# Sampled attention inside a hybrid decoder step: ranking moved behind the first keys, the near part closed early, last turns and page gates reordered

## The chip, the cores and the metric

The kernel runs on one core of one Trainium2 chip. The time is the device time of one execution in microseconds; lower is better.

## The reference

The program computes one inference step of a two-layer decoder for two groups that share the weights: one prompt of 256 tokens and 8 samples of 4 tokens with 2048 past tokens each. Each layer projects its input into a state-space group and an attention group of 8 query heads over 2 key/value heads. The attention has three branches: compressed blocks, the best 16 of 33 blocks of 64 past keys, and a window of 512. Cut to the selection and the three weighted sums:

```python
score = jnp.einsum('bktc,jc->bktj', p_cmp, overlap)
score = jnp.where(forced, FORCED_SCORE, jnp.where(causal, score, -1.0))
_, idx = lax.top_k(score, min(N_SEL, n_blocks))
...
o_slc = sel_attend(q, gather_selected_sample(cache_slc_kv, layer, page_table, kv_slc, idx), idx, pos)
...
o_win, _ = dense_gqa(q, kv_all[..., 0, :], kv_all[..., 1, :], d.astype(jnp.float32), (d >= 0) & (d < WINDOW))
...
attn = gates[..., 0:1] * o_cmp + gates[..., 1:2] * o_slc + gates[..., 2:3] * o_win
```

The samples' rows are the 128 combinations of sample, head of a key/value head, and step.

## The kernel before

The program is written by hand, one instruction stream for each engine, with semaphores between them; the order of the work is the order of the code. A loop runs the layer twice. In each layer come the input projection with the state-space scan, the compression of the cached pages (a long row of convolution matmuls), the attention stage that this change concerns, the output projection and the feed-forward network, whose matmuls (L1046) are most of TensorE's time.

In the attention stage TensorE, VectorE and ScalarE work on the prompt's 8 heads (two buffers, `a` and `b_`, heads in turn) and on the samples at once:

- **Keys.** Twenty sets of keys of about 1 MB or less, numbered 0 to 19, pass through a ring of four buffers. Sets 0 to 3 are the window's, 4 to 19 the past's 2048 positions. Even sets are asked for by SP, odd ones by GpSimd (POOL), eight pages of 128 KB each, when the set four places ahead has been used (`kring_free`). `keys(n, e)` (L869) multiplies set 2n+e into bank 2; VectorE's `window_out` and `keys_out` (L1669) add the position bias, write the result to SBUF and free the bank (`kgroup_evac`). The window's scores are the near part `SW` (2 x 544 columns), the past's are the far part `SS` (2 x 2080 columns), the compressed branch's are `SCM`.
- **Ranking.** VectorE counts for each of 33 blocks how many beat it, with ties broken by a table that GpSimd's queue loads (`tie_in`), and writes a mask of blocks (`RNK`, L1731 and L1733). TensorE spreads it over the rows in `mask()`, VectorE adds it in `masked(i)` to 512 columns at a time and takes their maximum.
- **Prompt heads.** For head n: `scores` on TensorE; `prompt_bias` on VectorE (L1743 to L1753: bias, maxima); `prompt_exp` on ScalarE; `prompt_scale` on VectorE (L1758 to L1768); `turn_p` on TensorE (8 transposes, L904 to L908) and `turned` on ScalarE (L1289 to L1291); `weigh` on TensorE (L917 to L921); `prompt_out` on VectorE (L1772) for two heads at once. `prompt_bias` of a head waits for `turn_p` of the head two before it.
- **End of the samples' scores.** `sample_exp` on ScalarE (L1296) makes the exponentials of `SW`, then of `SS`; VectorE gates and normalises them (L1837 to L1850); TensorE transposes them in 12 turns of up to two 128-column blocks (L980), ScalarE copies each turn to SBUF (L1316, L1320). Turns 0 to 8 hold the far part, the second half of turn 8 and turns 9 to 11 the near and the compressed one. Their order is the list `TURNS`, their banks go round a ring of six.
- **Values.** For each of the 8 samples (batches) b, TensorE multiplies the transposed weights by 16 pages of values and the window's values (L999). Three buffers hold the pages: the key ring, weight slot 0, and the memory of `SS` itself (index 1 in `VB`), which batch 2 is the first to use. SP, GpSimd and ScalarE each ask for a third of its pages (L354). Loads of later batches wait until the batch before them in the same buffer is done (`vring_free`). Between the batches TensorE sums squares for the two output norms (L571, L1025), which ScalarE makes. The output projection's first weights are loaded in the same stretch.

The order before: VectorE ranks right after the first window half. The near part's maximum, exponentials and scaling come at the very end, with the far part's, after head 7's scaling. ScalarE makes the far exponentials behind the evacuations of heads 6 and 7. TensorE turns heads 6 and 7, then three near turns, weighs heads 6 and 7, then does the nine other turns. Batch 2's pages wait for the last turn (`st_done` 12).

## Time and profile before

| | us |
|---|---|
| median of 3 runs | 3471.27 |
| lowest and highest | 3469.81, 3475.97 |
| the profiled execution, its own time | 3474.08 |
| span of its trace | 3472.5 |
| TensorE matmul busy in it | 3222.8 (93%) |
| VectorE busy | 1855.5 (53%) |
| ScalarE busy | 1232.9 (36%) |
| mean granted TensorE clock | 0.965 |

The attention stage lies at about 587 to 766 us in the first layer and 2314 to 2495 us in the second. A timeline row gives the start, the duration from there to the end of what is merged in it, the engine, the line, the operation with its tensors, and in square brackets how long the engine sat idle before it and what ended that. DVE is VectorE, ACT ScalarE, PE TensorE; a q behind a name is that engine's sequencer, which carries out waits, drains and DMA issues. The granted clock is a share of 2.4 GHz.

### The profile page before, as it was taken

To read this page: it belongs to the slowest core of one execution; us is meant where nothing else is said; L and a number is where in the kernel's file an instruction comes from. 1 tells how busy PE (TensorE), PEld (TensorE's weight loads), DVE (VectorE), ACT (ScalarE), POOL (GpSimd) and SP (SyncE) were. 2 spreads that over 40 slices of the span, in tenths; PEclk is the share of its full clock that TensorE was granted. 3 is DMA by queue.
4 is the path that set the end of the run, shared out by engine and by line. 5 is a ranking of instruction groups with operands and counts; after the bars stand their busy time and mean duration, and the time that the engine had idled before them with its cause. 6 is when DMAs were issued, how large, how long until landed. Compare 5 with 4: busy or idle time off the path is not lost. (4 is left out here: it accounts for less than half of the span.)

```text
span 3472.5 us, 56544 instructions
## 1 busy us (share of the span) xinstructions
PE 3222.8 (93%) x21882; PEld 2904.9 (84%) x21882; DVE 1855.5 (53%) x2703; ACT 1232.9 (36%) x1534; POOL 313.1 (9%) x556
## 2 busy tenths in 40 slices
PE   6899998769999999999979999987699999999998
PEld 4677777559999999999956777765599999999998
DVE  4887565734444444444448875656344444444444
ACT  2121453423333333333322124534233333333332
POOL 0001233430000000000000011324200000000000
PEclk8999999879999999999989999998899999999999
DMA  4524555764444444444234244656644444444443
GB/s 159 215 84 155 183 184 178 224 243 158 157 158 169 169 163 156 164 169 151 116 133 190 97 173 155 206 161 220 242 151 165 169 158 159 166 169 151 164 170 124
DMA packets 141468, 579.77 MB, mean 167 GB/s; under 512 B 21009, under 2 KB 91314, under 8 KB 115570
## 3 DMA queue, kind: packets, MB, share of 16 engines
q1 hardware_dynamic: 105282, 472.09, 36.9%
q0 software_dynamic: 26528, 76.84, 6.5%
q10 hardware_dynamic: 9488, 28.71, 2.1%
q8 instruction: 90, 1.47, 0.2%
q14 instruction: 80, 0.66, 0.1%
HBM read 570.02 MB, written 24.18 MB: 171 GB/s over the span
## 5 line engine op out<-in xcount | busy, mean ns | idle before, releaser
L1046 PE MATMUL banks<-normed_hi,weights_hi 128*128 128x288 f32 x4224 | 1251.5, 296 | 5.3 <-DVE ffn_hidden L1420 3.4
L1046 PE MATMUL banks<-normed_lo,weights_hi 128*128 128x288 f32 x4224 | 1246.1, 295 | 0.0
L1046 PE MATMUL banks<-normed_hi,weights_lo 128*128 128x288 f32 x4224 | 1241.9, 294 | 0.0
L1420 DVE TENSOR_TENSOR weights_lo<-weight_slots,weights_hi 128x2048 fp32r<-128x2048 f32 x296 | 686.7, 2320 | 990.9 <-ACTq L1345 990.4
L1342 ACT ACTIVATE weights_hi<-weight_slots 128x2048 fp32r<-128x2048 f32 x296 | 566.9, 1915 | 1101.1 <-PE banks L1046 1099.4
L1046 PEld LDWEIGHTS banks<-normed_hi,weights_hi 128*128 128x128 f32 x4224 | 791.5, 187 | 6.4 <-DVE ffn_hidden L1420 3.8
L1046 PEld LDWEIGHTS banks<-normed_hi,weights_lo 128*128 128x128 f32 x4224 | 795.5, 188 | 0.0
L1046 PEld LDWEIGHTS banks<-normed_lo,weights_hi 128*128 128x128 f32 x4224 | 792.9, 188 | 0.2
L646 PE MATMUL banks<-normed,weight_slots 128*128 128x288 f32 x1664 | 440.6, 415 | 8.9 <-DMA weight_slots<-in_w_in 8.9
L646 PEld LDWEIGHTS banks<-normed,weight_slots 128*128 128x128 f32 x1664 | 322.5, 195 | 103.0 <-issue 13.0
L835 PE MATMUL banks<-conv_high,conv_weights 128*128 128x508 f32 x1024 | 331.3, 405 | 14.3 <-DVE conv_low_b L1420 9.3
L835 PEld LDWEIGHTS banks<-conv_high,conv_weights 128*128 128x128 f32 x1024 | 192.6, 190 | 67.9 <-DVE conv_low_b L1420 16.1
L372 DVE TENSOR_TENSOR arena<-arena 128x256 f32<-128x256 f32 (+4 forms) x576 | 221.5, 388 | 29.8 <-issue 0.9
L1258 ACT ACTIVATE conv_high<-arena 128x512 fp32r<-128x512 f32 x256 | 157.9, 628 | 170.6 <-PE banks L835 170.4
L1046 PE MATMUL banks<-mixed_hi,weights_hi 128*128 128x288 f32 x512 | 158.3, 309 | 12.0 <-DVEq L1884 12.0
L339 POOL DMA_DIRECT2D arena<-in_cache_cmp x256 | 137.6, 538 | 282.6 <-issue 256.0
L1046 PE MATMUL banks<-mixed_lo,weights_hi 128*128 128x288 f32 x512 | 154.6, 302 | 0.0
L1046 PE MATMUL banks<-mixed_hi,weights_lo 128*128 128x288 f32 x512 | 154.0, 301 | 0.0
L1103 ACT ACTIVATE projected<-banks 128x576 f32<-128x576 f32 x28 | 18.2, 649 | 310.2 <-PE banks L646 290.9
L1420 DVE TENSOR_TENSOR conv_low_a<-arena,conv_high 128x512 fp32r<-128x512 f32 x128 | 86.5, 690 | 73.0 <-ACT conv_high L1258 71.7
L1420 DVE TENSOR_TENSOR conv_low_b<-arena,conv_high 128x512 fp32r<-128x512 f32 x128 | 87.6, 691 | 67.2 <-ACT conv_high L1258 65.9
L1046 PEld LDWEIGHTS banks<-mixed_hi,weights_hi 128*128 128x128 f32 x512 | 99.6, 195 | 13.3 <-issue 12.6
(298 smaller groups left out, 3036.3 us busy)
## 6 DMA issues: line engine op xcount, KB each, us to landing
weight_slots<-in_w_gu SPq DMA_DIRECT2D x88, 2048.0 KB, 7.5
weight_slots<-in_w_down SPq DMA_DIRECT2D x44, 2048.0 KB, 7.6
weight_slots<-in_w_in SPq DMA_DIRECT2D x28, 2048.0 KB, 8.3
arena<-in_cache_cmp SPq DMA_DIRECT2D x256, 128.0 KB, 4.1
arena<-in_cache_cmp POOLq DMA_DIRECT2D x256, 128.0 KB, 4.1
weight_slots<-in_w_out SPq DMA_DIRECT2D x16, 2048.0 KB, 7.6
out_win_kept<-in_win_rows ACTq DMA_DIRECT2D x2, 8128.0 KB
arena<-in_cache_slc_v SPq DMA_DIRECT2D x76, 128.0 KB, 5.1
```

The source lines that it names most:

```text
L339: eng.dma_start(AR[:, o:o + 256], T["cache_cmp"][bass.ds((lay * 160 + page) * 2 + k, 1)] .rearrange("a p x -> p (a x)")).then_inc(S[f"raw{ ...
L372: return eng.tensor_tensor(out, a, b, op)
L646: mm = pe.matmul(PS[s][:, m, 0:TOK], WR[:, s, c, 128 * m:128 * m + 128], hc(c), start=c == 0, stop=c == KC - 1)
L835: mm = pe.matmul(acc, w, x, start=i == hf == 0 and x is hi and w is wh, stop=i == 15 and hf == 1 and x is lo)
L1046: mm = pe.matmul(out, wt[:, hf, col], x[:, rhs + c, :], start=begin and c == 0 and i == 0, stop=hf == 1 and c == k - 1 and i == 2, skip_gr ...
L1103: act.activation(dst, src, ACT.Copy).then_inc(S[sem], by)
L1258: act.activation(HRG[:, n % 4, :].rearrange("p (g x) -> p g x", x=16), RAW[u % 2][:, :, i, :], ACT.Copy)\
L1342: w = act.activation(WH[:, hf, :], WR[:, s, 8 * hf:8 * hf + 8, :].rearrange("p a b -> p (a b)"), ACT.Copy)
L1420: return dve.tensor_tensor(out, a, b, op)
```

## The change

On VectorE, the ranking moves from behind the first window half to behind the second key part (the new function `rank`). The window's second half moves between heads 0 and 1. The near maximum is closed right behind it, and the gating of the compressed part and the scaling of the near part move from the end to between heads 2 and 3. The mask's copy moves behind `keys_out(1, 0)`. At the end, the far maximum is taken ahead of `prompt_out(4)` and the far part is scaled between heads 6 and 7. The instructions are the same, with one small reduction split in two.

On TensorE, `mask()` moves behind the first two heads' weighing, the three near turns move ahead of head 6's turn, and head 7's turn goes between far turns; both weighings follow the last turn. The turns' banks are a ring of four (0, 1, 4, 5), so that banks 6 and 7 stay with the heads. On ScalarE, the near exponentials follow those of heads 0 and 1, the far ones stand ahead of the evacuations of heads 6 and 7. The pages of batch 2 wait one by one for the turn that empties their columns.

```diff
+            TURNS = [9, 10, 11, 8] + list(range(8))
+            def turned_off(x):
+                ends = [(w - k * NS) // P // 2 for k, w in ((w // NS, w) for w in (256 * x, min(256 * x + 255, 2 * NS - 1)))]
+                return max(TURNS.index(n) for n in ends) + 1
...
-                if not last:
-                    eng.wait_ge(*((S["kring_free"], 22), (S["st_done"], 12), (S["kring_free"], 22))[VB[b]])
+                if not last and VB[b] != 1:
+                    eng.wait_ge(S["kring_free"], 22)
                 for x, page in zip(mine, p):
+                    if not last and VB[b] == 1:
+                        eng.wait_ge(S["st_done"], turned_off(x))
...
-            TURNS = [9, 10, 11] + list(range(9))
+            TURN_BANKS = [0, 1, 4, 5]
...
                 half_group(0, 0)
-                mask()
                 half_group(0, 1)
...
                 turn_and_weigh(0, ((1, 0),))
+                mask()
...
+                pe.wait_ge(S["ps_max"], NQ)
+                pe.wait_ge(S["sw_ready"], 1)
+                for i in range(3):
+                    turn_s(i)
+                turn_p(6, a)
+                pe.wait_ge(S["sw_ready"], 2)
+                for i in range(3, 8):
+                    turn_s(i)
+                turn_p(7, b_)
+                for i in range(8, 12):
+                    turn_s(i)
+                weigh(6, a, 1)
+                weigh(7, b_, 1)
...
+                prompt_exp(0, a)
+                prompt_exp(1, b_)
+                act.wait_ge(S["sw_max"], 1)
+                sample_exp(1, SW)
...
+                for i in range(3):
+                    turned_s(i)
+                act.wait_ge(S["sw_max"], 2)
+                sample_exp(0, SS)
+                turned(6, a)
+                for i in range(3, 8):
+                    turned_s(i)
+                turned(7, b_)
+                for i in range(8, 12):
+                    turned_s(i)
...
                 prompt_bias(0, a)
+                window_out(1)
                 prompt_bias(1, b_)
-                window_out(1)
                 dve.tensor_reduce(mxw[:, :, 0], SW[:, :, 0:WIN], AXX, ALU.max)
...
                 keys_out(0, 1)
+                rank()
                 prompt_bias(2, a)
+                gated_compressed()
+                for k in range(NKV):
+                    sample_scale(1, k, SW)
+                dve.drain().then_inc(S["sw_ready"], 1)
                 prompt_bias(3, b_)
                 keys_out(1, 0)
+                dve.wait_ge(S["mask_done"], 1)
+                dve.tensor_copy(MB, PS[3][:, :, 256:288])
...
+                dve.drain()
+                dve.tensor_reduce(SM[:, 54:56], mxs, AXX, ALU.max)
...
                 prompt_out(4)
                 prompt_scale(6, a)
+                for k in range(NKV):
+                    sample_scale(0, k, SS)
+                dve.drain().then_inc(S["sw_ready"], 1)
                 prompt_scale(7, b_)
+                prompt_out(6)
```

Two places in the instruction order. VectorE behind the first window half (the row of two 128x256 parts), before: the ranking, then head 0's bias.

```order
L1669 SCALAR_TENSOR_TENSOR arena<-consts,banks 128x256 x2
L1420 TENSOR_TENSOR arena<-arena 64x1089 x2
L1731 TENSOR_REDUCE arena<-arena 64x33
L1733 TENSOR_SCALAR arena<-arena 64x33
L1743 SCALAR_TENSOR_TENSOR weight_slots<-consts,banks 128x512
L1743 SCALAR_TENSOR_TENSOR weight_slots<-consts,banks 128x256
L1746 SCALAR_TENSOR_TENSOR weight_slots<-consts,banks 128x30
L1750 TENSOR_REDUCE smalls<-weight_slots 128x2 x3
L1753 TENSOR_SCALAR smalls<-smalls 128x6
```

VectorE after, from the second key part on (line numbers are those of the changed kernel: L1695 is the key part, L1759 to L1769 a head's bias, L1823 the gating, L1829 to L1835 the near part's scaling).

```order
L1695 SCALAR_TENSOR_TENSOR arena<-consts,banks 128x256 x2
L1446 TENSOR_TENSOR arena<-arena 64x1089 x2
L1812 TENSOR_REDUCE arena<-arena 64x33
L1814 TENSOR_SCALAR arena<-arena 64x33
L1759 SCALAR_TENSOR_TENSOR weight_slots<-consts,banks 128x512
L1759 SCALAR_TENSOR_TENSOR weight_slots<-consts,banks 128x256
L1762 SCALAR_TENSOR_TENSOR weight_slots<-consts,banks 128x30
L1766 TENSOR_REDUCE smalls<-weight_slots 128x2 x3
L1769 TENSOR_SCALAR smalls<-smalls 128x6
L1823 TENSOR_SCALAR arena<-arena,gates_sample 128x127 x2
L1829 TENSOR_SCALAR smalls<-smalls 128x1
L1831 RECIPROCAL smalls<-smalls 128x1
```

The ranking now stands three parts (a window half and two key parts), two head biases and two head scalings later, and the near part's scaling follows head 2's bias.

ScalarE at the end of the stage, before: near exponentials (544 columns), evacuations of heads 6 and 7, far exponentials (2080 columns), then the turns.

```order
L1296 ACTIVATE arena,smalls<-arena,smalls 128x544 x2
L1289 ACTIVATE weight_slots<-banks 128x512
L1290 ACTIVATE weight_slots<-banks 128x256
L1291 ACTIVATE weight_slots<-banks 15x256
L1289 ACTIVATE weight_slots<-banks 128x512
L1290 ACTIVATE weight_slots<-banks 128x256
L1291 ACTIVATE weight_slots<-banks 15x256
L1296 ACTIVATE arena,smalls<-arena,smalls 128x2080 x2
L1316 ACTIVATE arena<-banks 128x512
```

ScalarE after, the same place (L1321 and L1325 copy the samples' turns, L1309 makes the exponentials, L1302 to L1304 evacuate a head).

```order
L1321 ACTIVATE arena<-banks 128x512
L1325 ACTIVATE arena<-banks 128x256
L1325 ACTIVATE arena<-banks 32x256
L1321 ACTIVATE arena<-banks 127x256
L1309 ACTIVATE arena,smalls<-arena,smalls 128x2080 x2
L1302 ACTIVATE weight_slots<-banks 128x512
L1303 ACTIVATE weight_slots<-banks 128x256
L1304 ACTIVATE weight_slots<-banks 15x256
L1325 ACTIVATE arena<-banks 32x256
L1325 ACTIVATE arena<-banks 128x256
L1321 ACTIVATE arena<-banks 128x512 x4
```

The three near turns are copied ahead of the far exponentials, and head 6's evacuation now follows these.

## Rows read from the trace of the kernel before

**Rows 1.** Waits of TensorE over the whole span: us in total, times, longest.

```profile
PE banks L869 <- DVEq L1723: 27.6, 4, 12.4
```

**Rows 2.** Timeline of VectorE, first part of the stage; the last row is layer two.

```profile
602.49 2.65 DVE L1420 TENSOR_TENSOR arena<-arena 64x1089 f32<-64x1089 f32 x2 [3.62 <-DMA arena<-in_ties]
...
606.93 1.14 DVE L1743 SCALAR_TENSOR_TENSOR weight_slots<-consts,banks 128x512 f32<-128x512 f32 x2 [0.19 <-issue]
...
609.59 1.14 DVE L1743 SCALAR_TENSOR_TENSOR weight_slots<-consts,banks 128x512 f32<-128x512 f32 x2
...
621.65 0.87 DVE L1669 SCALAR_TENSOR_TENSOR arena<-consts,banks 128x256 f32<-128x256 f32 x2 [1.38 <-PE banks L869]
626.23 1.14 DVE L1743 SCALAR_TENSOR_TENSOR weight_slots<-consts,banks 128x512 f32<-128x512 f32 x2 [3.71 <-PE banks L908]
...
635.30 0.68 DVE L1772 COPY normed<-banks 128x512 f32<-128x512 f32 x1
...
2365.41 0.68 DVE L1772 COPY normed<-banks 128x512 f32<-128x512 f32 x1
```

**Rows 3.** Timeline of TensorE, key sets 4 to 7; the last row is layer two.

```profile
613.25 3.64 PE L869 MATMUL banks<-arena 128*32 128x256 f32 x32 [12.27 <-DVEq L1723]
...
618.00 3.58 PE L869 MATMUL banks<-weight_slots,arena 128*32 128x256 f32 x32 [0.54 <-DVEq L1779]
...
2340.84 3.64 PE L869 MATMUL banks<-arena 128*32 128x256 f32 x32 [12.36 <-DVEq L1723]
```

**Rows 4.** Single page loads of L327 on SP, each with its time to landing.

```profile
L327 SPq DMA_DIRECT2D arena<-in_cache_slc_k x1: 333/333/333, 596.0 to 596.0; - x1
...
DMA to landing us min/median/max: 12.4/12.4/12.4
...
L327 SPq DMA_DIRECT2D arena<-in_cache_slc_k x1: 333/333/333, 2323.4 to 2323.4; - x1
...
DMA to landing us min/median/max: 15.9/15.9/15.9
...
DMA to landing us min/median/max: 8.6/8.6/8.6
```

**Rows 5.** Timeline of VectorE, end of the samples' scores, first layer.

```profile
675.40 0.17 DVE L1832 TENSOR_SCALAR smalls<-smalls 128x4 f32<-128x4 f32 x1
...
679.75 0.48 DVE L1837 TENSOR_SCALAR arena<-arena,gates_sample 128x127 f32<-128x127 f32 x2
...
682.52 0.50 DVE L1850 TENSOR_SCALAR arena<-arena,smalls 128x544 f32<-128x544 f32 x1 [0.42 <-issue]
...
688.45 0.15 DVE L1844 TENSOR_SCALAR smalls<-smalls 128x1 f32<-128x1 f32 x1 [0.22 <-ACTq L1298]
```

**Rows 6.** Timeline of ScalarE, the first half of the far exponentials.

```profile
684.05 2.03 ACT L1296 ACTIVATE arena<-arena,smalls 128x2080 f32<-128x2080 f32 x1
```

**Rows 7.** Timeline of TensorE, turns, weighings and first batch; the last row is layer two.

```profile
677.57 0.47 PE L904 MATMUL banks<-consts,weight_slots 128*128 128x128 f32 x1 [8.01 <-DVEq L1768]
...
683.20 2.37 PE L980 MATMUL banks<-consts,arena 128*128 128x128 f32 x10 [0.39 <-DVEq L1853]
...
691.16 4.15 PE L980 MATMUL banks<-consts,arena 128*128 128x128 f32 x36 [1.12 <-DVEq L1853]
698.43 0.41 PE L999 MATMUL banks<-ssm_out,arena 127*32 127x128 f32 x4 [3.13 <-ACTq L1322]
...
702.96 5.25 PE L571 MATMUL banks<-squares,consts 128*128 128x288 f32 x16
...
2433.09 5.09 PE L571 MATMUL banks<-squares,consts 128*128 128x288 f32 x16 [1.47 <-ACT squares L566]
```

**Rows 8.** Stretches: length, busy us (count) PE, PEld, DVE, ACT, POOL, clock, DMA share, GB/s.

```profile
677.50:685.40 7.90, 6.12 (x27) 4.96 (x28) 4.14 (x18) 3.57 (x7) 0.00 (x0) 0.50 0.64 217
691.10:695.30 4.20, 4.14 (x36) 3.89 (x36) 0.00 (x0) 2.77 (x5) 0.00 (x0) 1.00 0.01 2
...
724.00:762.00 38.00, 21.02 (x385) 17.32 (x381) 3.12 (x7) 4.12 (x3) 8.72 (x12) 0.68 0.88 327
```

More of the change, by code:

```diff
@@ L1283, in prompt_exp @@
                     act.drain().then_inc(S["p_exp"], 1)
-                for j, h in enumerate(HEADS):
-                    prompt_exp(j, h)
                 def turned(n, h):
@@ L1298, in sample_exp, with turned_s @@
                         act.drain().then_inc(S["sw_exp"], 1)
-                for i in range(3):
-                    for j, h in enumerate(HEADS):
-                        turned(2 * i + j, h)
-                    for j, h in enumerate(HEADS):
-                        prompt_exp(2 * i + 2 + j, h)
-                act.wait_ge(S["sw_max"], 1)
-                sample_exp(1, SW)
-                for j, h in enumerate(HEADS):
-                    turned(6 + j, h)
-                sample_exp(0, SS)
                 widths = [P] * 16 + [SMP] + [P] * 4 + [SMP] + [NCMP]
-                for i, n in enumerate(TURNS):
+                def turned_s(i):
                     act.wait_ge(S["st_done"], i + 1)
+                    n = TURNS[i]
                     w = widths[2 * n:2 * n + 2]
-                    src = bank([0, 1, 4, 5, 6, 7][i % 6])
+                    src = bank(TURN_BANKS[i % 4])
                     if len(set(w)) == 1:
@@ L1322, in _ @@
                     act.drain().then_inc(S["st_evac"], 1)
+                a, b_ = HEADS
+                prompt_exp(0, a)
[3 more added lines that the diff above has]
+                for i in range(3):
+                    for j, h in enumerate(HEADS):
+                        turned(2 * i + j, h)
+                    for j, h in enumerate(HEADS):
+                        prompt_exp(2 * i + 2 + j, h)
+                for i in range(3):
+                    turned_s(i)
[7 more added lines that the diff above has]
+                    turned_s(i)
                 values(act, 2, "rest")
@@ L1725, in _ @@
                 window_out(0)
-                dve.wait_ge(S["tie_in"], 16)
-                tt(sel[1], sel[1], sel[2], ALU.mult)
-                dve.drain()
-                tt(sel[0], sel[0], sel[1], ALU.add)
-                dve.drain()
-                dve.tensor_reduce(RNK, sel[0], AXX, ALU.add)
-                dve.drain()
-                dve.tensor_scalar(RNK, RNK, float(NSEL), MASKED, ALU.is_ge, ALU.mult)
-                dve.drain().then_inc(S["ranked"], 1)
                 d1, dcp, slh = const(K_D1), const(K_DCP), const(K_SLH)
```

82 lines of the change are left out of this document (40 added, 42 removed).

## The prediction

> **What bounds the kernel now.** I read the waits of TensorE first, then the timelines of the attention stage, engine by engine. [rows 1]: over the two layers TensorE waits 27.6 us for one line of VectorE, L1723, the drain behind a window or key part. The timelines place it: per layer one wait of about 12.3 us before key set 4 [rows 3]; later one of 8.01 us before the seventh head's turns, and 3.13 us before the value products [rows 7]. VectorE is what TensorE waits for and is itself nearly full: from the third head's bias at 626.23 to the first head output at 635.30 there is no gap worth naming [rows 2]. So a removed TensorE wait is worth only what VectorE's own chain gets shorter. Times below are of the first layer; the second repeats them 1727.6 us later (the wait for set 4 ends at 613.25 and 2340.84), and 1730.1 later from 635.30 and 2365.41 on [rows 2, 3].
>
> **Early part: ranking and near part.** Before, VectorE waits 3.62 us for the tie table, ranks from 602.49 to 606.74 (4.25 us), and only then does heads 0 and 1 (2.66 us each, 606.93 to 609.59) and the second window half [rows 2]. In the new order, from 598.87 (602.49 less the wait): bias 2.7, window half 1.0, bias 2.7, the near maximum 1.7, scale 2.1, so VectorE is free at 609.1. The window half frees the key bank at 602.7 instead of 613.2, ten microseconds earlier.
>
> That is not the gain, because the keys are not there. Set 4's last page, issued at 596.0, lands 12.4 us later, at 608.4; in the second layer 2323.4 plus 15.9, 2339.3 [rows 4]. So TensorE starts it at 608.4 and 2339.3 against 613.25 and 2340.84: 4.8 and 1.5 us. Its 32 matmul records take 3.64 [rows 3], at the 1.2 GHz level ("cold" below, a granted clock of 0.50 as in the first of [rows 8]; 1.00 is 2.4 GHz, "warm"): done at 612.1 and 2342.9. Set 6's last page, issued at 605.4, lands 8.6 later, at 614.0 (the last line of [rows 4]). The next two sets take 3.58 us where they stood before [rows 3], done at 617.6 against 621.6; in the second layer I take 2.7, between 3.58 and a warm half of it, from 2343.9: 2346.6.
>
> Then VectorE: key part 1.0 (L1669, 0.87 and its drain), rank 4.25: 622.9 and 2351.9. Ranking now stands where VectorE before waited 3.71 us for the first turn (626.23) [rows 2]. From the end of set 7 to that turn's end it took 626.1 less 621.6, 4.5 us; from 617.6 that gives 622.1, so the turn is just ready and the rank hides in it. From 626.23 to 635.30 everything stays: 9.07 us. Added into it are the gating and the near part's two scalings, 679.75 to 683.02, 3.3 us [rows 5], and the mask's copy, 0.3 (an estimate from the 0.68 of the 512-column copy). Sum: 622.9 + 12.7 = 635.6 against 635.30, a **loss of 0.3**; second layer 2351.9 + 12.7 = 2364.6 against 2365.41, a **gain of 0.8**. The early rearrangement as a whole is about zero: VectorE is work-conserving there, and 3.3 us moved in uses up the waits taken out. Bounds: if the sets start no sooner than before, the loss is 3.7 per layer (rank 4.25 plus 3.6 less the 3.71 wait and about 0.4); if set 6 runs at the warm clock, a gain of 1.5. I take the middle since set 4's landing is a row. Behind 635.30 the order of VectorE is unchanged until the last mask add; that stretch keeps its length.
>
> **Late part.** The last maximum no longer waits for the head copy (0.68) and the near one: ready at 674.55 against 675.57 [rows 5]. ScalarE before did the near exponentials, then turns 6 and 7, and began the 2080-column exponential at 684.05 [rows 6]. Now near exponentials are long done and this one starts at 674.6, **9.4 us earlier**. Two halves at 2.2 each end at 676.8 and 679.0. VectorE has copied the heads and scaled head 6 (2.1, as from 675.5 to 677.57) at 677.3, and scales the halves, 1.95 each (688.45 to 690.4) [rows 5]: 679.3 and 681.3. TensorE did the three near turns (10 transposes) while VectorE masked, so they and their evacuations cost nothing; they are covered by the 8.01 us wait, of which 4 us would have to go before they showed. Head 6's turn (from 677.4, 1.9 us) ends before 681.3 too.
>
> From 681.4 on, TensorE's sum: 20 transposes of the far part, cold, 4.5 (10 took 2.37 at 683.20); head 7's turn, 8 transposes, 1.2, between 0.9 warm and 1.9 cold by the same two rows; 16 transposes warm 1.85 (36 took 4.15 at 691.16); the two last weighings 4.65 (685.4 to 690.04, partly cold) [rows 7]. That is 12.2: the value products start at 693.6 against 698.43. ScalarE is not later: before, its evacuations trailed the last transpose by 3.1 us (695.31 to 698.43), and now 4.65 us of weighing stand there. Gain **4.8**. The weighings and a turn, which lay in a gap before, now stand in the path: that is why 9.4 shrinks to 4.8. Then the first batch: it took 4.53 us (698.43 to 702.96) after its 3.13 us wait, but 3.1 in the second layer (698.43 plus 1730.1 to 2431.6), which then waited 1.47 for squares until 2433.09 [rows 7]. Now there is no wait ahead (TensorE comes warm) and ScalarE's squares are 7 us earlier, so both layers save 1.45 more. **Late gain 6.25 per layer**, 12.5 in all. Bounds: all warm (2.3 + 0.9 + 1.85 + 4.15, with the batch's 1.45) 9.3 per layer; all cold (4.7 + 1.9 + 3.8 + 7, the weighings estimated as 1.5 times theirs here) about zero.
>
> **The bank ring** shrinks from six to four; ScalarE's pace was 0.8 a turn (691.16 to 698.43, nine turns), under the 0.9 of four cold transposes, so it costs nothing above this sum. **The gates of the value pages** free pages 0 and 3 some 5 us before the last turn, the rest with it. In the old trace nobody waits for the third batch's pages: they were asked from 695.5 and used at 717.66; now they are asked by 689 and wanted near 711. I price the gates at zero; cover is the 20 us of batches 0 and 1.
>
> **What follows.** Every later load is released by a batch that TensorE has finished, so its release moves with TensorE. From 724 to 762 the DMA engines are 88% busy at 327 GB/s [rows 8]. The Trainium skill, page "Trainium Kernel Development and Optimization", Key Constraints, says that DMAs of SP, ACT and POOL "all run on the same 16 DMA engines and interleave"; by that rule earlier issue by itself cannot shorten this tail, only an earlier start can. The trace agrees with that reading at 88%, and the sum does not rest on it: the start is earlier here. The FFN behind it is unchanged.
>
> **Sum.** 12.5 + 0.8 - 0.3 = 13.0 us. The profiled execution took 3474.1 (span 3472.5); it gives 3461. Against the median of 3471.27 it gives **3458**.
>
> **Rivals.** A: the early part loses its bound. Sets 6 and 7 or the turns come later than I reckon and VectorE's added 3.3 us is paid fully, 3.7 per layer. For it: VectorE's density, and landings of 12.4 and 15.9 us that show a crowded DMA [rows 4]. Against: sets 4 to 7 are asked at the same times as before. 13.0 less (3.4 + 4.5) leaves 5: **3466**.
>
> B: the tail gives it back. The value pages and output weights of the last four batches take the DMA's time whatever TensorE does, and the gain ends as a longer wait for pages. For: [rows 8]. Against: at 88% it has some room, and each page is asked when TensorE has freed its place, so the whole tail starts earlier. Only the warm batch and 1 to 2 us remain: **3469**.
>
> C, slower: TensorE's clock. The new order leaves TensorE idle from about 671 to 677 and again for 2 us before the long row of transposes. If it then stays at the 1.2 GHz level to the first batch, the late path has 17.4 us instead of 12.2 and no gain; if set 6, the score products and first turns are cold too (3.5 us later than reckoned), the early part loses 3.8 and 2.7. It decides from the point where both the transposes and the weighings run cold: 3471.3 + 6.5 = **3478**. For it: from 677.5 to 685.4 the granted clock is 0.50, after 8 us of idling [rows 8]. Against: one row of weighings later, from 691.1 to 695.3, it is 1.00, in spite of 1.1 us of idling between [rows 7, 8]. The Trainium skill, "TensorE: Matmul & The Clock Gate", Part 1, says that "the default state is throttled, and activity releases the throttle", which speaks against the longer idling here; by it the long transposes would start cold, which is what I charge, and then warm. The trace agrees: 10 transposes in 2.37 at 0.50 and 36 in 4.15 at 1.00 [rows 7, 8].
>
> **How the numbers follow.** Forecast 0.64 (3452 to 3464); A 0.18 (3463 to 3469); B 0.10; C 0.08. A measurement of this kernel tells about 0.2% (7 us) from no change: faster is below 3464.3, the forecast and half of A, 0.73; same is half of A, B and a little of C, 0.20; slower 0.07. For 8 in 10 the range takes the forecast with its warm bound (3449) and most of A: 3449 to 3469.
>
> **What would show it.** Right: set 4's keys start at landing, near 608 and 2339, not at 603; the first head output near its old place (within 1.5 us); the 2080-column exponential about 9 us earlier; value products 4 to 7 us earlier; waits for value pages of the old size. Wrong: a VectorE gap before the third head's bias (A), longer page waits in the tail (B), transposes and weighings at the clock of 1.2 GHz throughout (C). If the first head output comes 3 us or more earlier, I have overcharged the moved near part.

## The result and the profile after

The changed kernel took 3458.01 us (median of 10 runs, 3450.33 to 3465.15) against 3473.16 us for the kernel before (10 runs beside them, 3469.81 to 3477.86): a ratio of 0.9954, with a 95% interval of 0.9946 to 0.9963. Run once more on another chip, it gave 0.9945 [0.9933, 0.9957]. The forecast of 3458 us holds. The profiled execution took 3458.01 us, with a span of 3456.4 against 3472.5 before, 16.1 us less.

Waits of TensorE in the changed kernel over the whole span, those of the attention stage that matter here (waited for: us in total, times, longest us):

```profile
PE banks L1014 <- DMA arena<-in_cache_slc_v: 18.6, 6, 8.5
PE banks L878 <- DVEq L1795: 15.2, 6, 3.8
PE banks L913 <- DVEq L1784: 13.5, 2, 6.7
PE banks L878 <- DMA arena<-in_cache_slc_k: 12.9, 2, 7.5
...
PE banks L1014 <- DMA weight_slots<-in_cache_slc_v: 8.7, 2, 4.5
...
PE banks L981 <- DVEq L1892: 4.1, 2, 2.1
...
PE banks L878 <- DMA weight_slots<-in_win_k: 2.6, 1, 2.6
...
PE banks L878 <- DMA weight_slots<-in_cache_slc_k: 1.9, 1, 1.9
...
PE banks L878 <- DVEq L1749: 1.5, 1, 1.5
```

Of the 27.6 us of [rows 1] 1.5 are left (L1749 is the old L1723). In their place TensorE waits 14.8 us for key pages, where it waited 2.4 before, and 2.6 us for a window page. The waits for value pages are what they were, 27.3 us in sum against 28.0. L878 is the old L869, L1014 the old L999, L981 the old L980.

Timeline of TensorE in the changed kernel, first layer: start of the stage (L859) and key sets 4 to 7, the lines that answer to [rows 3] (start us, us, engine and line, operation, and in brackets the idle time before it and what ended it). A row of 32 records holds two key sets, and is called here by the first of them: "set 4" is sets 4 and 5, "set 6" is 6 and 7.

```profile
589.91 1.08 PE L859 MATMUL banks<-projected,arena 128*32 128x127 f32 x32 [0.70 <-issue]
...
611.37 3.64 PE L878 MATMUL banks<-arena 128*32 128x256 f32 x32 [5.38 <-DMA arena<-in_cache_slc_k]
616.13 3.64 PE L878 MATMUL banks<-weight_slots,arena 128*32 128x256 f32 x32 [1.12 <-DVEq L1795]
```

The stage starts at 589.91 here and at 587.16 in the execution before (2310.48 and 2314.32 in the second layer), so I count from that start. Set 4 begins at 21.46 instead of 26.09. VectorE, the lines that answer to [rows 2] and [rows 5] (ranking's reduction, first head output, last maximum):

```profile
623.55 1.28 DVE L1812 TENSOR_REDUCE arena<-arena 64x33 f32<-64x1089 f32 x1
...
637.26 0.68 DVE L1788 COPY normed<-banks 128x512 f32<-128x512 f32 x1
...
676.58 0.17 DVE L1887 TENSOR_SCALAR smalls<-smalls 128x2 f32<-128x2 f32 x1
```

The first head output stands at 47.35 against 48.14 us from the stage's start, and in the second layer at 48.07 against 51.09. ScalarE and TensorE at the end of the stage, the lines that answer to [rows 6] and [rows 7]:

```profile
676.78 2.03 ACT L1309 ACTIVATE arena<-arena,smalls 128x2080 f32<-128x2080 f32 x1 [1.28 <-DVE smalls L1887]
```

```profile
671.34 1.31 PE L981 MATMUL banks<-consts,arena 128*128 128x128 f32 x10
...
683.42 4.45 PE L981 MATMUL banks<-consts,arena 128*32 128x128 f32 x20 [2.08 <-DVEq L1892]
...
689.22 1.91 PE L981 MATMUL banks<-consts,arena 128*128 128x128 f32 x16
...
695.13 0.41 PE L1014 MATMUL banks<-ssm_out,arena 127*32 127x128 f32 x4
```

Stretches of the changed kernel (length, busy us of PE, PEld, DVE, ACT, POOL with counts, clock, DMA share, GB/s):

```profile
683.40:688.20 4.80, 4.78 (x23) 4.72 (x24) 1.80 (x8) 2.73 (x6) 0.54 (x1) 0.50 0.23 79
689.20:691.00 1.80, 1.80 (x19) 1.80 (x18) 0.00 (x0) 1.48 (x4) 0.53 (x1) 1.00 0.18 57
```

The reader sees the far exponential 86.87 us from the stage's start instead of 96.89. Twenty transposes follow at a granted clock of 0.50 (1.2 GHz), 0.22 us each, and then sixteen at 1.00 (2.4 GHz), 0.12 us each. The value products begin at 105.22 against 111.27. Nothing is given back later: the output projection starts at 172.14 against 179.05, and at 170.05 against 180.99 in the second layer. The two layers save 6.91 and 10.94, 17.85 in sum; the rest of the program differs by 1.8 us the other way.

### The profile page after: what moved, and what is told of

Its sections match the earlier page's. It is cut to its first block, busy times and chain, and to the rows that moved or that the text cites. A ratio compares the mean times of both kernels' runs of the same rounds, so it can differ in the third digit from the quotient of the medians.

```text
span 3456.4 us, 56548 instructions
## 1 busy us (share of the span) xinstructions
PE 3225.8 (93%) x21882; PEld 2905.8 (84%) x21882; DVE 1857.0 (54%) x2705; ACT 1233.0 (36%) x1534; POOL 313.2 (9%) x556
## 4 chain that ended last, share of the span: by engine, by line
PE 42%; DVE 3%; DMA 2%; ACT 1%; issue 1%; DVEq 1%; ACTq 0%; SPq 0%; PEld 0%; PEldq 0%
PE banks L1061 27%; PE banks L655 5%; PE banks L844 4%; DMA weight_slots<-in_w_in 1%; PE banks L645 1%; PE banks L632 1%; DMA arena<-in_cache_slc_v 1%; PE banks L878 1%; DMA weight_slots<-in_cmp_w 0%; DVE arena L1446 0%; DVE weights_lo L1446 0%; DMA weight_slots<-in_cache_slc_k 0%; PE banks L624 0%; PE banks L693 0%; PE banks L1014 0%
## 5 line engine op out<-in xcount | busy, mean ns | idle before, releaser
L381 DVE TENSOR_TENSOR arena<-arena 128x256 f32<-128x256 f32 (+4 forms) x576 | 221.7, 388 | 29.9 <-issue 0.9
```

The lines of the kernel that those rows point to most:

```text
L381: return eng.tensor_tensor(out, a, b, op)
```

## The experiments

Places below are microseconds from the start of the stage, first layer and second, each read from the profiled execution of the kernel: the first head output, the first 80 value products of a batch, and the start of the output projection. Ratios are against the kernel before on the same chip. (The value products that began at 105.22 and 111.27 above are the batch's first four records; its row of 80 follows 0.7 us later.)

| kernel | ratio, 95% interval | first output | value products | projection |
|---|---|---|---|---|
| before | 1 | 48.1, 51.1 | 112.0, 114.9 | 179.1, 181.0 |
| changed | 0.9954 [0.9946, 0.9963] | 47.4, 48.1 | 105.9, 106.3 | 172.1, 170.1 |
| e0_changed_again | 0.9945 [0.9933, 0.9957] | 46.7, 47.9 | 106.2, 108.8 | 171.1, 174.8 |
| e1_rank_first | 0.9977 [0.9967, 0.9986] | 52.5, 50.4 | 111.9, 108.9 | 176.5, 173.9 |
| e2_early_alone | 0.9996 [0.9987, 1.0004] | 48.6, 48.7 | 112.2, 112.4 | 177.4, 177.5 |
| e3_gates_back | 0.9951 [0.9939, 0.9964] | 51.0, 48.2 | 109.2, 106.4 | 173.4, 170.8 |
| e4_near_in_wait | 0.9956 [0.9941, 0.9972] | 44.7, 44.5 | 105.2, 103.3 | 171.3, 167.2 |
| e5_kept_warm | 0.9967 [0.9955, 0.9979] | 47.0, 47.7 | 102.8, 103.5 | 172.8, 173.1 |
| e6_table_later | 0.9961 [0.9948, 0.9975] | 49.0, 48.5 | 108.4, 106.4 | 173.0, 170.4 |
| e9_near_mid_warm | 0.9945 [0.9932, 0.9959] | 44.8, 44.2 | 101.4, 101.0 | 168.3, 166.0 |
| e10_all_warm | 0.9928 [0.9915, 0.9942] | 44.4, 44.9 | 98.7, 99.1 | 163.5, 163.2 |
| e11_kept_warm_fewer | 0.9961 [0.9948, 0.9973] | 49.4, 48.5 | 107.3, 106.2 | 175.1, 172.2 |
| e12_early_mid_warm | 0.9918 [0.9905, 0.9931] | 44.9, 45.2 | 101.9, 101.9 | 168.6, 167.9 |
| e13_all_warm_again | 0.9916 [0.9902, 0.9931] | 45.7, 44.7 | 99.7, 98.7 | 163.9, 163.8 |

The changed kernel once more on another chip, as a measure of what two executions differ by:

> The changed kernel once more, unchanged, on the chip of the next two runs, as what they are compared with. Theory: ratio to the kernel before 0.9954 within 0.0008. Rival (the gain depends on the chip): a ratio outside 0.9945 to 0.9963.

Measured: 0.9945, at the edge between the two; 3456.7 us against 3458.0. The two executions agree within about 1 us in the first layer and differ by 2.6 us at the second layer's value products and by 4.8 at its projection. Part of the 2.6 is seen: in the second layer of the repeat set 12 followed a wait of 2.44 us and took 3.56, where it took 1.94 in the changed kernel. So a single place is read to 3 to 5 us, and only durations and waits of single rows, and the time between two neighbouring rows, are read closer.

**The ranking's place.** `rank()` goes back ahead of the first heads' scores, and the near part stays early:

```
                 window_out(0)
+                rank()
...
                 keys_out(0, 1)
-                rank()
                 prompt_bias(2, a)
```

> The changed kernel with the ranking back at its old place, right behind the first window half; all else as changed. My theory (VectorE is work-conserving in the early part, and the ranking's new place fills the wait for the third head's turn): the window half frees the key bank some 8 us later, set 4 starts near 613 instead of near 611 and the ranking no longer fills VectorE's wait, so each layer is 3 us longer: about 6 us over the changed kernel, ratio to the kernel before 0.9970 to 0.9975. Rival (keys were bound by their landing, the move gives nothing): the same time as the changed kernel, 0.995. Rival (the move is where all the early gain comes from, set 4's start moves 5 us and passes through): 10 us, 0.998 or more.

Measured: 0.9977, and the wait for VectorE before set 4 is back. TensorE of e1_rank_first:

```profile
612.75 3.19 PE L878 MATMUL banks<-arena 128*32 128x256 f32 x32 [9.41 <-DVEq L1749]
620.21 3.64 PE L878 MATMUL banks<-weight_slots,arena 128*32 128x256 f32 x32 [4.27 <-DVEq L1808]
```

The first output comes 5.2 and 2.3 us later than in the changed kernel. The interval, 0.9967 to 0.9986, excludes the first rival (0.995) and not the second (0.998). Moving the ranking behind the keys is therefore worth about half of the whole change, as long as the near part stands early.

**The early part alone.** Ranking and near part as in the changed kernel, but the last turns on ScalarE and TensorE and the end of VectorE's order as before: the far scaling and its signal stand behind the last head's, and the far maximum behind `prompt_out(4)`. On VectorE, against the changed kernel:

```
+                prompt_out(4)
...
-                prompt_out(4)
                 prompt_scale(6, a)
+                prompt_scale(7, b_)
                 for k in range(NKV):
                     sample_scale(0, k, SS)
+                prompt_out(6)
                 dve.drain().then_inc(S["sw_ready"], 1)
-                prompt_scale(7, b_)
-                prompt_out(6)
```

> The kernel before with the early part of the change alone: ranking behind the second key part, near maximum, near exponentials, gating and near scaling early, the mask's product behind the first weighings; the end of the stage in the old order (heads 6 and 7 turned and evacuated, then the far exponentials, six banks, pages of batch 2 at the last turn). My theory as predicted: the early part gives about zero up to the first head output, and as the trace of the changed kernel shows it, 0.8 us in the first layer and 3.0 in the second; nothing after it but the near maximum's 0.2 us. So about 4 us under the kernel before, ratio 0.9985 to 0.9995. Rival (the near part's 3.3 us was on the end's path before, and its leaving the end is a gain of its own): another 3 us or more per layer, ratio 0.997 or less.

Measured: 0.9996, no change; the rival, a gain of its own at the stage's end, is out. The first output is at its old place in the first layer (48.57 against 48.14) though TensorE starts set 4 at 21.74 instead of 26.09; in the second it comes 2.4 us earlier (48.72 against 51.09), no more than two executions differ by. This was the prediction's claim: the ranking's removal from the wait pays for the 3.3 us of near part moved in, and no more. The two experiments fit together if the ranking's move is the cover of the near part: without it (e1_rank_first) the first output is 4.4 us later than before the change in the first layer, though 0.7 earlier in the second. The late part alone was not run, so what the late order brings is the difference between this run and the whole change, 0.9996 to 0.9954, and not a run of its own.

**The gates.** Page gates of the value loads as before:

```
-                if not last and VB[b] != 1:
-                    eng.wait_ge(S["kring_free"], 22)
+                if not last:
+                    eng.wait_ge(*((S["kring_free"], 22), (S["st_done"], 12), (S["kring_free"], 22))[VB[b]])
...
-                    if not last and VB[b] == 1:
-                        eng.wait_ge(S["st_done"], turned_off(x))
```

> The changed kernel with the page gates of batch 2 undone: all its pages wait for the last turn again. My theory: nobody waits for these pages, the cover is the 20 us of batches 0 and 1, so the same time as the changed kernel, ratio 0.995 to 0.996. Rival (the early pages take load from the crowded tail): 2 us or more slower than the changed kernel, and longer waits for pages in batches 4 to 7.

Measured: 0.9951 against 0.9954 for the change: the gates turn by turn are worth nothing that can be measured. The value products of the third batch did not wait for pages in either, in either layer.

**The near part in a real gap.** In the changed kernel VectorE idles before the last keys of the middle pair of heads (`keys_out(2, 1)`), 2.67 us in the first layer and 3.76 in the second (the expectation says 3.8 for both). The near scaling goes there:

```
-                gated_compressed()
-                for k in range(NKV):
-                    sample_scale(1, k, SW)
-                dve.drain().then_inc(S["sw_ready"], 1)
                 prompt_bias(3, b_)
...
                 keys_out(2, 0)
+                gated_compressed()
+                for k in range(NKV):
+                    sample_scale(1, k, SW)
+                dve.drain().then_inc(S["sw_ready"], 1)
                 keys_out(2, 1)
```

> The changed kernel with the gating and the near part's scaling moved from between heads 2 and 3 to just ahead of VectorE's write of the key sets 14 and 15, where VectorE waits 3.8 us for TensorE in both layers. My theory (VectorE's chain sets the early part, each us of work in it counts and work in a wait is free): the third head's chain up to the first head output is 2.9 us shorter per layer and the moved work vanishes in the wait: 5 to 6 us faster than the changed kernel, ratio 0.9937 to 0.9942. Rival (TensorE or the key landings bound the stretch once VectorE is lighter): under 2 us gained, ratio 0.995. Rival (the work lands in front of a bank that TensorE waits for): slower than the changed kernel.

Measured: 0.9956, a miss; nothing was gained beyond the change. The timeline of TensorE tells where it went. First e4_near_in_wait, the key sets of the middle (10, 12 and 14), then the same sets in the changed kernel:

```profile
630.72 1.93 PE L878 MATMUL banks<-weight_slots,arena 128*32 128x256 f32 x32 [0.19 <-DVEq L1795]
...
639.44 3.51 PE L878 MATMUL banks<-arena 128*32 128x256 f32 x32 [2.13 <-DVEq L1795]
...
647.75 3.64 PE L878 MATMUL banks<-weight_slots,arena 128*32 128x256 f32 x32 [3.78 <-DVEq L1795]
```

```profile
634.46 3.58 PE L878 MATMUL banks<-weight_slots,arena 128*32 128x256 f32 x32 [2.55 <-DVEq L1795]
...
643.50 1.93 PE L878 MATMUL banks<-arena 128*32 128x256 f32 x32 [0.92 <-DVEq L1795]
...
650.23 2.45 PE L878 MATMUL banks<-weight_slots,arena 128*32 128x256 f32 x32 [3.78 <-DVEq L1795]
```

The granted clock in sets 12 and 14 of e4_near_in_wait, then in set 12 of the changed kernel (length, busy us of PE, PEld, DVE, ACT, POOL with counts, clock, DMA share, GB/s):

```profile
639.50:642.90 3.40, 3.40 (x33) 1.50 (x33) 2.52 (x7) 0.00 (x0) 0.00 (x0) 0.53 0.28 94
647.80:651.30 3.50, 3.50 (x32) 1.49 (x32) 2.16 (x10) 2.41 (x12) 0.51 (x1) 0.50 0.74 248
```

```profile
643.50:645.40 1.90, 1.90 (x33) 1.12 (x33) 1.81 (x4) 0.23 (x1) 0.00 (x0) 1.00 0.75 233
```

The stages start at 588.80 and 589.91. Set 12 of e4_near_in_wait begins at 50.64, 2.95 us ahead of the changed kernel's (53.59). But it follows a wait of 2.13 us instead of 0.92 and takes 3.51 us instead of 1.93, so it ends 1.37 ahead; set 14 takes 3.64 instead of 2.45 and ends 0.18 ahead. The time won on VectorE became a longer idle on TensorE, and the slower matmuls behind it used it up. In the second layer sets 12 and 14 took 2.77 and 3.30 us, and of 4.1 us of lead at set 12 3.0 were kept to the value products. That is no more than two executions differ by.

**TensorE kept busy in the middle.** To e4_near_in_wait, transposes of the identity whose results nobody reads are added in the waits before sets 12 and 14. They write bank 6, so they wait until ScalarE has emptied it. `keep_on` is new:

```
+                def keep_on(count, n=2):
+                    for x in range(count):
+                        pe.transpose(bank(n)[:, 128 * (x % 4):128 * (x % 4) + 128], ident, ident)
...
-                turn_and_weigh(1, ((2, 0), (2, 1)))
+                turn_p(2, a)
+                pe.wait_ge(S["pt_evac"], 4)
+                keep_on(8, 6)
+                half_group(2, 0)
+                turn_p(3, b_)
+                pe.wait_ge(S["pt_evac"], 5)
+                keep_on(20, 6)
+                half_group(2, 1)
+                weigh(2, a, 0)
+                weigh(3, b_, 0)
```

> The kernel with the near block of the sampled heads moved into the wait ahead of the last keys of set group 2 (label e4_near_in_wait), and in it 8 and 20 transposes of the identity into bank 6 (read by nobody) ahead of the two key sets between turn_p(2) and weigh(2). In e4_near_in_wait the first key set of the stretch came 2.95 us earlier from the stage's start than in the changed kernel, but the two sets took 3.51 and 3.64 us behind waits of 2.13 and 3.78 us, against 1.93 and 2.45, and the lead was 1.37 us behind the one and 0.18 us behind the other. My theory (the 1.2 GHz clock after these waits takes the lead back): both sets take 1.93 us, the value products start 2 to 2.9 us earlier from the stage's start than in e4_near_in_wait (105.2 and 103.3 us there), ratio about 0.9940. Rival (VectorE's own work between the sets sets the pace, and faster sets only make TensorE wait longer for the bank): the sets take 1.93 us, the waits ahead grow by as much, value products within 0.7 us of e4_near_in_wait, ratio 0.9955.

Measured: the sets take 1.93 us each, with no wait between the added transposes and set 14; the granted clock of both is 1.00 (second block):

```profile
639.95 1.93 PE L878 MATMUL banks<-arena 128*32 128x256 f32 x32
...
644.13 2.40 PE L937 MATMUL banks<-consts 128*128 128x128 f32 x20 [1.23 <-ACTq L1320]
646.68 1.93 PE L878 MATMUL banks<-weight_slots,arena 128*32 128x256 f32 x32
```

```profile
640.00:641.80 1.80, 1.80 (x33) 0.86 (x32) 1.72 (x4) 0.00 (x0) 0.00 (x0) 1.00 0.50 172
646.70:648.60 1.90, 1.90 (x33) 1.14 (x33) 1.53 (x9) 1.90 (x9) 0.54 (x1) 1.00 0.93 314
```

The value products come at 101.4 and 101.0 instead of 105.2 and 103.3: 3.8 and 2.3 us, about as expected. The ratio of 0.9945 overlaps the 0.9956 of e4_near_in_wait, and these places overlap what executions differ by; what carries the verdict is the time from row to row. From the start of set 12 to that of set 14 it is 6.73 to 6.74 us in every execution of this order in which set 12 took 1.93 to 1.94, and 8.31 to 8.37 in those in which it ran slow (both layers of e4_near_in_wait, the second of e0_changed_again); e9_near_mid_warm is back at 6.73 and 6.74. From set 14 to set 16 it is 6.13 and 6.12 us here against 8.60 and 7.49. The two stretches give 4.05 us back in the first layer and 3.00 in the second. The clock, then, and not VectorE, took the lead back: had VectorE set the pace, as the rival says, the starts would not have moved.

**TensorE kept busy before the far turns.** On the changed kernel:

```
                 for i in range(3):
                     turn_s(i)
+                pe.wait_ge(S["kgroup_evac"], 11)
+                keep_on(40)
                 turn_p(6, a)
+                keep_on(16)
```

> The changed kernel, with 40 transposes of the identity into a free bank (their result is read by nobody) between the first six near and cached turns of the sampled heads and turn_p(6), and 16 more behind turn_p(6), so that TensorE does not idle before the 20 far transposes. In the changed kernel those 20 took 4.45 us behind waits of 2.08 us, and 16 behind them 1.91 us. My theory (the clock level after an idle is what they cost): the 20 take about 2.4 us, the value products start 2.0 us earlier in each layer, ratio to the kernel before about 0.9942 (changed kernel alone 0.9954). Rival one (ScalarE and VectorE, which empty the banks of the turns, set the pace): the transposes get faster but wait in between, the value products start no more than 0.5 us earlier, ratio 0.9953. Rival two (the added transposes are still running when the far scores are ready): the value products start later, ratio 0.996 or more.

Measured: 0.9967, no better than the change and above its interval at the middle, though the transposes did what was expected. TensorE, then ScalarE of e5_kept_warm:

```profile
680.66 2.36 PE L981 MATMUL banks<-consts,arena 128*32 128x128 f32 x20 [1.20 <-DVEq L1901]
...
690.33 2.39 PE L1023 MATMUL banks<-arena 128*32 128x128 f32 x80
695.10 6.47 PE L580 MATMUL banks<-squares,consts 128*128 128x288 f32 x16 [2.37 <-ACT squares L575]
```

```profile
690.43 4.12 ACTq L363 DMA_DIRECT2D arena<-in_cache_slc_v  x5
694.60 0.78 ACT L575 ACTIVATE squares<-normed 128x288 f32<-128x288 f32 x2 [5.85 <-issue]
```

The transposes took 2.36 us for 4.45, and the value products came 3.1 and 2.7 us earlier. Then TensorE waited 2.37 and 2.50 us for the squares, and both normalisations ran slow (6.47 and 6.41 us where the changed kernel has 5.09; the granted clock over the first was 0.73 for 1.00). ScalarE's page issues began only 2.2 and 1.8 us earlier than in the changed kernel, since its evacuations now bind, and the five of them took 4.12 and 4.25 us in place of 2.42, which used up what was left. The lead is gone at the second batch: it began at 114.0 and 114.8, the changed kernel's at 113.3 and 113.6. The third batch's row of 80 (the expectations below call it the second batch) began at 126.2 and 127.0, against 124.6 and 123.8 in the changed kernel and 125.0 and 127.7 in its repeat, so that it came later than without the added transposes is not shown. Both rivals of the expectation were wrong about the place: the cost was behind the value products, in ScalarE's queue.

**Fewer of them.** The same with `keep_on(30)` and `keep_on(8)`.

> e5_kept_warm with 30 and 8 added transposes instead of 40 and 16. In e5_kept_warm the 20 far transposes took 2.36 us instead of 4.45 and the value products started 3.1 and 2.7 us earlier from the stage's start, but ScalarE's third value-page issue behind them took 2.03 us, where one took 0.5 in every other kernel, with an instruction packet on the DMA queues in that microsecond, in both layers; its squares came 2.4 us late, the normalisation ran at 1.2 GHz and the second batch began 1.6 and 3.2 us later than in the changed kernel. Theory one (the stall belongs to where ScalarE's code lies, which the added TensorE instructions do not move): it is there again, at 4.1 us for the five issues, ratio 0.9965. Theory two (it belongs to the moment, the code packet and the pages meeting on the queues): with other timing the five issues take 2.4 us again, the value products still start 2 us or more earlier if 38 transposes are enough to hold the clock, ratio 0.9945 or lower.

Measured: 0.9961. The twenty transposes took 3.32 and 3.48 us, so with 38 added ones instead of 56 they ran at 2.4 GHz only in part. The value products came no earlier. The issues took 3.46 us in the first layer and 2.43 in the second, where theory one wanted 4.1 in both and theory two 2.4 in both. Neither holds as it stands: the stall is not fixed to the code, and it does not vanish with another timing.

**The table's place on SyncE.**

```
-                sp.wait_ge(S["w2_done"], 10)
-                sp.dma_start(CT[:, at[2]:at[2] + 2048], ...)
                 for t in range(4, 20, 2):
                     key_set(sp, t)
+                    if t == 4:
+                        sp.wait_ge(S["w2_done"], 10)
+                        sp.dma_start(CT[:, at[2]:at[2] + 2048], ...)
```

> The changed kernel with one edit: SyncE issues the load of the 1024 KB of tables behind the pages of key set 4 instead of ahead of them. In the changed kernel TensorE waits 5.4 and 7.5 us for the landing of set 4 and then 1.1 and 1.9 us at set 6. My theory (the early part is bound by the pages' landings, and the DMA engines are near full there, so that an order changes who lands first and not the amount): set 4 lands up to 3 us earlier, set 6 as late as now, the first head's output is within 1 us of now, ratio 0.9954 within 0.0005. Rival one (what counts is set 4 alone): the first head's output comes 2 us or more earlier in each layer, ratio 0.9942. Rival two (VectorE waits for the tables before it scales the first head): first output 2 us later, ratio 0.9965.

Measured: 0.9961 [0.9948, 0.9975], which holds the expected 0.9954 and also the 0.9965 of rival two, but not the 0.9942 of rival one. Its key sets 4 and 6:

```profile
606.90 3.64 PE L879 MATMUL banks<-arena 128*32 128x256 f32 x32 [5.37 <-DMA arena<-in_cache_slc_k]
615.51 3.64 PE L879 MATMUL banks<-weight_slots,arena 128*32 128x256 f32 x32 [4.97 <-DMA weight_slots<-in_cache_slc_k]
```

With the stage's start at 587.71, set 4 begins 2.3 us earlier than in the changed kernel, set 6 1.6 us later (27.80 against 26.22), and the first output 1.6 later, where at most 1 was expected; in the second layer it is 0.4 later. VectorE did wait 2.08 us for the tables, as rival two says, but it then idled 4.03 us until set 6 was done, so the tables were not what was waited for last. In the early stretch a page that lands earlier was paid for by another that landed later: after the change TensorE waits there for landings, and this order of the loads won nothing.

**All of it together.** e9_near_mid_warm, e5_kept_warm, and behind the window's last keys (sets 2 and 3) `keep_on(44, 6)`, behind set 4 `keep_on(12, 6)`.

> The edits of e9_near_mid_warm and e5_kept_warm together, and 44 transposes of the identity behind the second key set and 12 behind set 4, in TensorE's waits for the landing of pages. Set 4 and set 6 took 3.64 us each there. My theory: the gains add, 2 us of the far turns, 2 to 2.9 of the middle and 1 of the early sets (only set 4's last columns are waited for, set 6 still waits for its landing), ratio 0.9925 to 0.9932. Rival: each gain is taken by the next wait (landing of set 6, VectorE in the middle, the landing of the value pages at the stage's end), ratio no lower than 0.9940.

Measured: 0.9928 at 3443.6 us against 3469.4, within what the adding of the gains would give. The profiled execution of e10_all_warm, where TensorE comes to set 4:

```profile
603.26 5.02 PE L937 MATMUL banks<-consts 128*128 128x128 f32 x44
609.99 1.93 PE L878 MATMUL banks<-arena 128*32 128x256 f32 x32 [1.71 <-DMA arena<-in_cache_slc_k]
```

Set 4 takes 1.93 us for 3.64, the far turns took 2.35, and ScalarE's five issues 2.42, without the stall of e5_kept_warm. TensorE still waited 0.65 us for the squares in both layers, so of the 2.37 us of e5_kept_warm about 0.65 go to ScalarE's other work and 1.7 to the longer issues. Then the late part was taken out again:

> e10_all_warm without its late part: near block in the wait, added transposes in the early and the middle waits, none between the near and the far turns. e10_all_warm had 0.9928, e9_near_mid_warm (middle alone) 0.9945. Theory (the late transposes give 2 us per layer, the early ones 1): ratio 0.9938 to 0.9942, the 20 far transposes back at 4.45 us. Rival (the early ones carried it): 0.9930 or lower.

Measured: 0.9918, on the rival's side, though the twenty transposes stood at 4.45 us again and the third batch started 5 and 4 us later than in e10_all_warm. As the two had not run side by side, e10_all_warm was repeated:

> e10_all_warm once more, unchanged, on another chip, since e12_early_mid_warm (0.9918 [0.9905, 0.9931]) and e10_all_warm (0.9928 [0.9915, 0.9942]) were not run beside one another. In the traces the second batch of value products starts 117.0 and 117.4 us behind the stage's start in e10_all_warm and 122.1 and 121.6 us in e12_early_mid_warm. Theory (the late transposes are worth what the traces say, some 4 us per layer): 0.9900 to 0.9915. Rival (the ratios are right and the late transposes are worth nothing over the other two): 0.9918 to 0.9930.

Measured: 0.9916 (3442.4 us against 3471.4), just between the two expected ranges. The traces agree with one another (projection at 163.9 and 163.8 us, as in e10_all_warm, against 168.6 and 167.9 in e12_early_mid_warm), the ratios do not tell the kernels apart. In the medians e12_early_mid_warm is 2.4 and 3.6 us slower, but the three runs were on three chips, on which the kernel before had 3474.5 (e12), 3469.4 and 3471.4. Whether the late transposes are worth anything on top of the other two stays open. That the whole beats both kernels is shown: its ten times run from 3439.5 to 3449.9 us with medians of 3443.6 and 3442.4, the sixteen of the changed kernel from 3450.3 to 3465.2 with medians of 3458.0 and 3456.7.

## Why the prediction was right, point by point

**The wait for VectorE and what takes its place.** Right. Set 4 started at landing, at 21.46 from the start where the prediction had 21.2 (608.4 less 587.16). In the second layer it had 25.0 from a landing of 15.9 us [rows 4] and the trace shows 21.37, with the page landed 3.6 us earlier. That time was one execution's: where set 4 waited for its landing in this order, the waits ran from 5.4 to 10.6 us.

**The early part is worth about nothing.** Right in kind: e2_early_alone, 0.9996. In size: the first layer came out 0.8 us better where the prediction had 0.3 worse, the second 3.0 better where it had 0.8. Set 6 was through at 29.9 and 30.5 us from the start, where the prediction had 30.4 and 32.3, which would cover 0.6 of the 1.1 us and 1.8 of the 2.2; but these are places of one execution, so that the landings made the difference is argued and not shown. VectorE's density was read rightly: the ranking lies where it had waited for the first turn [rows 2]. The prediction charged sets 4 and 6 at about 3.6 us each (set 6 of the second layer at 2.7, where it took 3.64). What it missed is set 10: the near part put ahead of VectorE's write of the sets before it made TensorE wait 2.55 and 3.04 us, and set 10 ran at 3.58 and 3.64 us where it had taken 1.94 and 1.93. In this execution that cost nothing that shows: from the first output to the last maximum it is 39.3 and 39.5 us, and it was 40.1 in both layers (40.3 and 41.8 in e0_changed_again).

**The late part.** Right, term by term. The far exponentials moved by 10.0 us (9.4 forecast). The twenty transposes took 4.45 (4.5) and 4.24 to the next start, the eight of head 7's turn 1.56 (1.2), the sixteen 1.75 to the next start (1.85), the weighings 4.16 (4.65), from start to start 11.7 for 12.2. The largest miss among the terms of this sum is the weighings' 0.5. The first batch took 3.01 us to the squares for 3.08. From the first output to the squares of the normalisation the stage shrank by 6.8 and 7.2 us; the forecast was 6.25.

**Gates and ring at nothing.** Right for the gates (e3_gates_back). The ring was not tried alone; ScalarE waited 0.21 to 0.26 us for each cold turn in the changed kernel, so it was not late there.

**The tail moves along.** Right: the projection moved by 6.91 and 10.94 us for 7.57 and 10.20 at the squares. Rival B, which gave the gain to the page waits, had 0.10; those waits are 27.3 us over both layers where they were 28.0. Rival A, in which VectorE pays the added 3.3 us in full, did not come, as the first output stands no later than before. Rival C was half right: TensorE's clock did fall before the twenty transposes and was back at 2.4 GHz for the sixteen behind them, as the forecast had charged. The Trainium skill's sentence in "TensorE: Matmul & The Clock Gate", Part 1, that activity releases the throttle, agrees with these two rows at 0.50 and 1.00.

**The sum.** 13.0 us forecast; 15.2 between the medians and 16.1 between the spans. The missing 2 to 3 us are about the 1.1 and 2.2 us by which the early part came out better. That 3458 was met to the microsecond is luck: the gain was 2.2 us larger than forecast, and the kernel before, with 3471.3 from three runs, had 3473.2 in the ten beside the changed one, 1.9 us more.

## What to carry to other kernels

When a wait is removed, look at what the waited-for engine does next: here VectorE was the path; what the early moves won they spent on the near part, and the gain came from the far work that could then be started earlier. TensorE's idle time had a second price in this stage, the slow matmuls behind it, and a step moved into a gap of one engine can lengthen the gap of another and be paid back in clock; with transposes that nobody reads in the waits, the same move brought its gain. Test such a filler with what follows it, since the next engine (here ScalarE and its page issues) may take it all.

## What the runs showed of the hardware

Behind a longer idle time the same key sets ran slower. In the kernels with no transposes added ahead of them, sets of the middle (10, 12 and 14) behind waits of 0.2 to 1.9 us took 1.93 to 1.94 us, those behind 2.1 to 2.6 us took 2.77 to 3.60, those behind 3.0 to 3.3 us took 3.64, and those behind 3.8 to 4.1 us from 2.41 to 3.64. The runs give no rule beyond that. The same wait of 3.78 us stood before 2.45 in one layer of the changed kernel and 3.54 in the other, and what came before the wait counts too: set 6 behind 1.12 us took 3.64, after a set 4 that had run at 3.64 itself.

Five page issues of 128 KB on ScalarE took 2.42 us in the changed kernel and in e10_all_warm, 3.49 and 3.64 in e12_early_mid_warm and 4.1 to 4.3 in e5_kept_warm, from the same line. In e5_kept_warm, e12_early_mid_warm and the slow one of e11_kept_warm_fewer's two (3.46 and 2.43) a packet of instructions stood on the DMA queues in the same microseconds; in e10_all_warm and e13_all_warm_again one did too, in the last tenths of the stretch, without a delay. So the packet was not shown to be the cause, and the stall stays open.
